# K/V token projections and output-gate projection placed inside the mLSTM chunk loop of a hybrid decoder layer

## What is computed

```python
proj = h @ w_in + b_in              # split: xin, bg, cg, q, k, v, o, ig, fg, gate_c, gate_m
y_conv = bg * causal_dwconv(cg * xin, conv_mix_w);  p_conv = y_conv @ w_proj_conv
# mLSTM, for each head and chunk, with decays from ig (exp) and fg (log_sigmoid):
#   C_next = s_old * C + sum_s w_s k_s v_s^T                  (state, carried from chunk to chunk)
#   num    = (tri * weights * q k^T) v + s_inter * (q C);     den: the same with v = 1
hm = num / max(|den|, exp(-m))      # then RMS norm over each head
hm = sigmoid(o) * rmsnorm(hm)
z = sigmoid(gate_c) * p_conv + sigmoid(gate_m) * (hm @ w_proj_mlstm)
x = x + gt1 * (z @ w_out)           # then a gated ConvFFN and a final norm
```

## Time and profile before

| | us |
|---|---|
| median of 2 runs | 1942.44 (1940.79 to 1944.08) |
| profiled execution | 1940.48 |
| its longest span, core 4, first to last instruction | 1939.2 |
| spans of the other seven cores | 1907.6 to 1935.8 |
| mean granted TensorE clock, core 4 | 0.857 of full |

### The profile page before, as it was taken

How to read it: one execution, slowest core, us unless ns; L and a number is a source line. 1 busy time by engine, 2 the same in 40 slices (tenths; PEclk the granted TensorE clock), 3 DMA queues, 4 the chain that set the end, 5 groups by cost and what they waited for, 6 DMA issues and landing times.

```text
span 1939.2 us, 25748 instructions; the slowest of 8 cores (1907.6 to 1939.2 us)
## 1 busy us (share of the span) xinstructions
PE 1494.9 (77%) x8664; PEld 802.5 (41%) x8664; DVE 950.2 (49%) x1746; ACT 651.0 (34%) x1436; POOL 118.0 (6%) x144
## 2 busy tenths in 40 slices
PE   0599649649987996297399979996296399979995
PEld 0254214325443443154256635553153255635553
DVE  0154472356245777123554356677123554256677
ACT  0253022533225333415422243323416322243333
POOL 1001000001000000100000000000100000100000
PEclk9699658759998998598599989998597599979998
DMA  4955932705776651927035594731936044684731
GB/s 96 166 137 94 156 66 44 109 1 84 112 121 108 93 83 44 205 45 109 1 52 80 88 171 62 114 56 59 209 47 100 1 66 66 100 154 72 110 55 66
DMA packets 142245, 174.54 MB, mean 90 GB/s; under 512 B 5155, under 2 KB 124963, under 8 KB 142117
## 3 DMA queue, kind: packets, MB, share of 16 engines
q0 software_dynamic: 131456, 136.86, 47.3%
q1 hardware_dynamic: 10662, 36.03, 5.5%
HBM read 301.35 MB, written 8.39 MB: 160 GB/s over the span
## 4 chain that ended last, share of the span: by engine, by line
PE 59%; DVE 14%; DMA 10%; issue 8%; ACT 7%; DVEq 1%; ACTq 0%; SPq 0%; POOLq 0%
PE psum L436 36%; PE psum L958 7%; PE psum L543 6%; DMA xt<-xin 3%; PE psum L535 3%; DMA wslot<-w_in 2%; DMA wslot<-w_ada 2%; PE psum L559 2%; PE psum L922 2%; ACT sqj L394 2%; DVE t3f L987 1%; DVE hm L789 1%; DVE C L562 1%; ACT t3f L985 1%; DVE actT L996 1%
## 5 line engine op out<-in xcount | busy, mean ns | idle before, releaser
L436 PE MATMUL psum<-hT,wslot 128*128 128x512 bf16 (+2 forms) x4800 | 773.9, 323 | 21.1 <-ACT hT L421 14.0
L436 PEld LDWEIGHTS psum<-hT,wslot 128*128 128x128 bf16 x4800 | 442.1, 100 | 340.3 <-issue 47.1
L958 PE MATMUL psum<-wslot,actT 128*128 128x512 bf16 x748 | 169.7, 388 | 22.4 <-DVE actT L996 22.0
L416 PE MATMUL psum<-identb,xnb 128*128 128x128 bf16 x392 | 38.6, 258 | 139.5 <-DVE stat L400 60.0
L961 DVE TENSOR_TENSOR x<-psum,x 128x512 f32<-128x512 f32 x204 | 133.9, 687 | 12.2 <-PE psum L958 1.2
L958 PEld LDWEIGHTS psum<-wslot,actT 128*128 128x128 bf16 x748 | 73.2, 99 | 116.1 <-issue 36.9
L894 ACT ACTIVATE sg<-psum,bcol 128x512 bf16<-128x512 f32 (+1 forms) x96 | 53.8, 563 | 177.4 <-PE psum L436 159.2
L978 ACT ACTIVATE a_s<-psum 128x512 f32<-128x512 f32 (+2 forms) x132 | 55.7, 470 | 150.9 <-DVE a_s L976 133.8
L991 ACT ACTIVATE sl<-t3f 128x768 f32<-128x768 f32 (+1 forms) x66 | 53.3, 808 | 142.6 <-DVE t3f L989 142.6
L119 POOL DMA_DIRECT2D wslot<-w_in x51 | 44.7, 883 | 913.5 <-PE psum L436 657.1
L416 PEld LDWEIGHTS psum<-identb,xnb 128*128 128x128 bf16 x392 | 29.5, 115 | 151.0 <-issue 150.8
(11 more groups left out here) (170 smaller groups left out, 1806.9 us busy)
## 6 DMA issues: line engine op xcount, KB each, us to landing
wslot<-w_in POOLq DMA_DIRECT2D x51, 1024.0 KB, 15.5
wslot<-w_up POOLq DMA_DIRECT2D x30, 1024.0 KB, 9.0
xt<-xin SPq DMA_DIRECT2D x49, 512.0 KB, 6.6
wslot<-w_down POOLq DMA_DIRECT2D x15, 1024.0 KB, 9.3
wslot<-w_ada POOLq DMA_DIRECT2D x12, 1024.0 KB, 24.1
y<-x SPq DMA_DIRECT2D x16, 512.0 KB, 2.7
wslot<-w_proj_conv POOLq DMA_DIRECT2D x6, 1024.0 KB, 11.7
wslot<-w_proj_mlstm POOLq DMA_DIRECT2D x6, 1024.0 KB, 10.8
```

The lines of the kernel that those rows point to most:

```text
L416: S.op("pe", lambda e, k=k, kk=kk: e.matmul(psum[:, b, kk * 128:(kk + 1) * 128], lhsT=xnb[i][:, k * 128:(k + 1) * 128], rhs=identb[:], sta ...
L436: S.op("pe", lambda e, k=k: e.matmul(psum[:, b, 0:n], lhsT=wslot[si][:, k, wcol0:wcol0 + 128], rhs=hT[:, k, t0:t0 + n], start=(k == 0), st ...
L958: S.op("pe", lambda e, jj=jj: e.matmul(psum[:, b, :], lhsT=actT[:, jj, c * 128:(c + 1) * 128], rhs=wd[:, jj, i * 512:(i + 1) * 512], start ...
```

## The change

In each stage the K/V block is taken apart. The 8 gate matmuls of each chunk stay ahead of `gate_math`, now in a loop of their own. The 24 matmuls of k and v (`kv_tok`) are issued for chunk 0 ahead of the output-gate units inside the gate stretch, and for chunk i+1 at the top of iteration i of the chunk loop. The output-gate units are cut finer: one for each 128 features and block of positions (16 instead of 8); 7 of the first block stay in the gate stretch, the other 9 are issued in the loop between `st_B` and `st_C2`: those that are due (the block holds the chunk) and, where there are any left, two more in each iteration. To leave banks 6 and 7 for this work, `st_B` uses 2 banks instead of 4 for its heads, with one ACT copy of 257 columns after each head instead of one of all four; the state update moves to banks 3 and 4 and the transposes to bank 5. The five weight slots of k, v and o are freed at the loop's end.

```diff
+        def gate_proj(hTt, r_hT, col0, gbank, ridx):
+            for k in range(8):
...
+        def kv_gate_proj(c, hTt, r_hT, col0, si_k, si_v, ktok, r_ktok, vaug, r_vaug, gbank, ridx, do_gate=True):
...
                     si_v = [load_w("w_in", O_V + i * 512) for i in range(2)]
+                    si_o = [load_w("w_in", O_O + i * 512) for i in range(2)]
                     for c in range(nch):
-                        kv_gate_proj(c, hT, r_hT[c], c * 128, si_k, si_v, ktok, r_ktok, vaug, r_vaug, gbank, c)
-                    free_w(si_k, *si_v)
+                        gate_proj(hT, r_hT[c], c * 128, gbank, c)
...
+                    def kv_tok(c):
+                        kv_gate_proj(c, hT, r_hT[c], c * 128, si_k, si_v, ktok, r_ktok, vaug, r_vaug, gbank, c, do_gate=False)
+                    o_units = []
+                    for (t0, n) in tbs:
+                        for j in range(8):
+                            def unit(t0=t0, n=n, j=j):
...
+                                fm_proj(si_o[j // 4], (j % 4) * 128, hT, r_hT, [(t0, n)], ev_o)
+                            o_units.append((t0 // 128, unit))
                     state["resv"] = {6, 7}
...
+                    pre_units = [lambda: kv_tok(0)] + [u_ for (_, u_) in o_units[:7]]
+                    o_units = o_units[7:]
+                    interleave(gate_math(ms, graw, r_graw, nch, first, True, (6, 7), gm), pre_units)
...
+                    def emit_o(due_chunk, extra):
+                        nonlocal_units = o_units
+                        while nonlocal_units and nonlocal_units[0][0] <= due_chunk:
+                            nonlocal_units.pop(0)[1]()
+                        for _ in range(extra):
+                            if nonlocal_units:
+                                nonlocal_units.pop(0)[1]()
+                    state["resv"] = {0, 1, 2, 3, 4, 5}
...
                         for h in range(4):
-                            S.op("pe", lambda e, h=h: e.matmul(psum[:, 1 + h, 0:257], lhsT=Sm[j][:, h, :], rhs=vaug[:, c, h, :], start=True, stop=False),
-                                 reads=[r_Sm[j], r_vaug[c]], writes=[r_X[h]], inc=False)
...
-                        S.op("act", lambda e: e.activation(out=Xs[j][:], in_=psum[:, 1:5, 0:257], func=AF.Copy), reads=r_X, writes=[r_Xs[j]])
-                        state_update(c, c * 4, ktok, r_ktok, vaug[:, c], r_vaug[c], sold, rg, (5, 6))
+                            xb = 1 + h % 2
+                            S.op("pe", lambda e, h=h: e.matmul(psum[:, xb, 0:257], lhsT=Sm[j][:, h, :], rhs=vaug[:, c, h, :], start=True, stop=False),
+                                 reads=[r_Sm[j], r_vaug[c]], writes=[r_X[h % 2]], inc=False)
+                            S.op("pe", lambda e, h=h: e.matmul(psum[:, xb, 0:257], lhsT=qT[:, h, cs], rhs=Cb[:, h, :], start=False, stop=True),
+                                 reads=[r_qT[c], r_Cb[h]], writes=[r_X[h % 2]])
+                            S.op("act", lambda e, h=h: e.activation(out=Xs[j][:, h, :], in_=psum[:, xb, 0:257], func=AF.Copy),
+                                 reads=[r_X[h % 2]], writes=[r_Xs[j]])
+                        state_update(c, c * 4, ktok, r_ktok, vaug[:, c], r_vaug[c], sold, rg, (3, 4))
...
                     for i in range(nch + 1):
                         if i + 1 < nch:
+                            kv_tok(i + 1)
                             prescale(i + 1)
                         if i < nch:
                             st_A(i)
                         if i >= 1:
                             st_C1(i - 1)
                         if i < nch:
                             st_B(i)
+                        emit_o(i, 2)
                         if i >= 1:
                             st_C2(i - 1)
                             st_D(i - 1)
+                    emit_o(nch, 99)
+                    free_w(si_k, *si_v)
+                    free_w(*si_o)
```

More of the change, by code:

```diff
@@ L530, in gate_math @@
             out.update(wG=wG, sold=sold, dmin=dmin, rg=rg)
-        def kv_gate_proj(c, hTt, r_hT, col0, si_k, si_v, ktok, r_ktok, vaug, r_vaug, gbank, ridx):
+        def gate_proj(hTt, r_hT, col0, gbank, ridx):
+            for k in range(8):
+                S.op("pe", lambda e, k=k: e.matmul(psum[:, gbank, ridx * 8:ridx * 8 + 8], lhsT=hTt[:, k, col0:col0 + 128], rhs=wgate[:, k, :],
+                                                  start=(k == 0), stop=(k == 7)),
+                     reads=[r_hT, r_wgate], writes=[r_bank[gbank]], inc=(k == 7))
+        def kv_gate_proj(c, hTt, r_hT, col0, si_k, si_v, ktok, r_ktok, vaug, r_vaug, gbank, ridx, do_gate=True):
             b = next_bank()
@@ L550, in kv_gate_proj @@
                      reads=[r_bank[b], r_par], writes=[r_vaug[ridx]])
[L551 to L554, removed]
+            if do_gate:
+                gate_proj(hTt, r_hT, col0, gbank, ridx)
         def state_update(ridx, gi0, ktok, r_ktok, vw, r_vw, sold, rg, pbank):
@@ L702, in run_stage @@
                          reads=[r_bank[gbank], r_par], writes=[r_graw])
-                    state["resv"] = {6, 7}
[L704 to L718, removed]
+                    def kv_tok(c):
+                        kv_gate_proj(c, hT, r_hT[c], c * 128, si_k, si_v, ktok, r_ktok, vaug, r_vaug, gbank, c, do_gate=False)
@@ new lines, in run_stage, with ev_o @@
+                    o_units = []
+                    for (t0, n) in tbs:
+                        for j in range(8):
+                            def unit(t0=t0, n=n, j=j):
+                                def ev_o(b, t0_, n_, j=j):
+                                    S.op("act", lambda e: e.activation(out=sgoT[:, j, t0_:t0_ + n_], in_=psum[:, b, 0:n_], func=AF.Sigmoid,
+                                                                       bias=bcol[:, 48 + j:49 + j]),
+                                         reads=[r_bank[b], r_par], writes=blk(r_sgoT, t0_, n_))
+                                fm_proj(si_o[j // 4], (j % 4) * 128, hT, r_hT, [(t0, n)], ev_o)
+                            o_units.append((t0 // 128, unit))
@@ L719, in run_stage @@
+                    state["resv"] = {6, 7}
                     gm = {}
-                    interleave(gate_math(ms, graw, r_graw, nch, first, True, (6, 7), gm), units)
+                    pre_units = [lambda: kv_tok(0)] + [u_ for (_, u_) in o_units[:7]]
+                    o_units = o_units[7:]
+                    interleave(gate_math(ms, graw, r_graw, nch, first, True, (6, 7), gm), pre_units)
                     wG, sold, dmin, rg = gm["wG"], gm["sold"], gm["dmin"], gm["rg"]
@@ L731, in run_stage @@
                     prescale(0)
-                    r_X = RL("X", 4)
+                    def emit_o(due_chunk, extra):
[6 more added lines that the diff above has]
+                    state["resv"] = {0, 1, 2, 3, 4, 5}
+                    r_X = RL("X", 2)
                     r_STb = Res("STb")
@@ L797, in st_D @@
                         for half in range(2):
-                            tb_ = 7
+                            tb_ = 5
                             for kk in range(4):
@@ L820, in run_stage @@
                             st_D(i - 1)
+                    emit_o(nch, 99)
+                    free_w(si_k, *si_v)
+                    free_w(*si_o)
+                    state["resv"] = set()
                     S.barrier()
```

2 lines of the change are left out of this document (removed).

## The result

| | us |
|---|---|
| median of 9 runs | 2004.94 (2000.44 to 2018.53) |
| the kernel before, beside it | 1942.27 (1938.72 to 1945.28), 8 runs |
| ratio | 1.032, 95% interval 1.0308 to 1.0331 |
| longest span of the profiled execution, core 5 | 2003.9 |
| forecast | 2014, range 1966 to 2060 |

The changed kernel is 62.7 us slower; +72 was forecast. In some executions of a kernel one die of the chip ran at a lower clock than the other; these are left out of the medians and ranges that follow, which is why some rest on one to three runs.

A forecast was written before the change was run, and what follows sets the result against it. PE's matmuls bound the K/V blocks, the chain the gate stretch, waits the loop. Terms: 162.1 in, 90.0 out, +72 us on the 1939.2 span gives 2011; plus 1.3 and 2.0, 2014 us, range 1966 to 2060.

The forecast's parts named there:

- all three items on which it would have been wrong: Loop signs: prescale waits under 1 us; state update no later behind the square root; clock near 0.5 or 1.0.
- bursts in iteration 0 (3): K/V matmuls in each loop's first iteration, after the gate stretch's idle tail: 7.1 us each.
- bursts in iteration 1 (3): K/V matmuls right behind output units that have raised the clock: 5.1 us each.
- bursts behind two units (6): K/V matmuls behind two output units and transposes, clock taken as midway: 6.25 us each.
- two banks: In st_B, head 2 waits for head 0's ACT copy behind the square root: +2.5 us in 14 iterations, 36.1 in all.
- new table loads: Sigmoids in the loop make the next square root reload its table: 7 x 1.28 = 9.0 us.
- output units in the loop: Unhidden in iteration 0, partly hidden later by the wait before the transposes: 30.4 us, bounds 18 and 42.
- out: K/V block less gate matmuls: Front of the stages: 91.6 us of K/V blocks go, 7.8 us of gate matmuls stay, 83.8 us saved.
- out: gate stretch: Shorter units and sigmoids against added kv_tok(0): about -1.0 us per 6 chunks, -4.2 for 5, -6.2 together.
- Full clock throughout: Loop: PE's clock stays full since it has more to do; +24, 1966 us; chance 0.13.
- Half clock throughout: Loop: the clock never rises inside it; +138, 2081 us; chance 0.10.
- Real overlap: Loop: new work fills PE's idle time, a burst costing only its DVE copies; -16, 1927 us; chance 0.05.

The follow-up runs named there:

- banks_only: The kernel before with only st_B put on two PSUM banks, one ACT copy after each head: 1974.72 us, ratio 1.0161.
- the last version: The run fill: changed kernel with K/V in three groups where PE waits, later DVE copies and a reordered loop; 1897.45 us, ratio 0.9777.
- o_dense: The changed kernel with all 16 output-gate units in the gate stretch, none in the loop: 2007.32 us, ratio 1.0322.
- fill: Changed kernel, K/V in three groups where PE waits, copies later, loop reordered, output units in gate stretch: 1897.45 us, ratio 0.9777; rerun 1889.51 and 1890.7.
- fill_dense: The run fill with all K/V projections in one block ahead of the gate stretch, the rest kept: 1954.28 us, ratio 1.0067.

## Why the forecast was right, and where its sizes were off

The direction, the mechanisms and all three items on which it would have been wrong came out as foretold: `prescale` waited for the copies of the burst, the state update moved behind the square root, and the loop's clock stood at 0.70. The terms, forecast against measured in the changed kernel's rows (for the bursts the forecast is the cost, length less 0.1 us, and the measured value the length):

| term | forecast | measured |
|---|---|---|
| bursts in iteration 0 (3) | 21.3 | 7.14 + 6.87 + 7.94 = 21.9 |
| bursts in iteration 1 (3) | 15.3 | 3 x 5.18 = 15.5 |
| bursts behind two units (6) | 37.5 | 5 x 5.18 + 6.99 = 32.9 |
| the stage of 5: the other two | 12.5 | 5.18 + 6.55 = 11.7 |
| two banks | 36.1 | 14 x 2.39 = 33.5 (iteration 0 under 0.2 each) |
| new table loads | 9.0 | 7 x 1.28 = 9.0 |
| the three loads of before, now on the chain | 0 | 3 x 1.17 = 3.5 |
| output units in the loop | 30.4 | 15.8 + 1.8 + 9.5 = 27.1 |
| in, sum | 162.1 | 155.1 |
| out: K/V block less gate matmuls | 83.8 | 91.6 - 3.4 = 88.2 |
| out: gate stretch | 6.2 | 3.4 + 1.5 + 1.1 = 6.0 |
| net | +72 | +61 by terms; spans +64.7, medians +62.7 |

**Bursts.** The term that was mis-sized upward: "the six behind two units and transposes 6.25, midway". Five of the six ran at full clock, 5.18. I had put them between two rows; what the changed timeline shows is that behind the 16 matmuls of the units and the transposes (from 947.56 to the next burst at 952.66, with one idle stretch of 0.94) the clock is up when the burst begins. The sixth, in the second stage of 6 (1531.26 to 1538.25), took 6.99 behind the same units; why is open. The run with all units in the gate stretch shows the other side: behind the first of each loop, bursts of 6.2 to 7.8 us. So -4.6 us here, and -0.8 in the stage of 5.

**Gate matmuls alone.** 7.8 us came from their weight loads inside the K/V block, 8 in 0.46, 57 ns each. Alone, 48 matmuls with their 48 loads take 1.35 us (867.12 to 868.47), 28 ns each: 4.4 us less over the three stages. The row gave the pace of loads with other matmuls around them.

**A term put at nothing.** "Before there was one such load in a loop": the sum counts only the seven new ones. In the kernel before, that one load was hidden, as the earlier trace rows shows together with the state update beside it:

```profile
911.29 0.88 DVE L562 SCALAR_TENSOR_TENSOR C<-C,g_sold,psum 128x257 f32<-128x257 f32 x2 [1.83 <-PE psum L559]
```

The state update began 0.42 us ahead of the load (911.71). In the changed kernel the same load stands before the copy of head 0, and the state update comes behind both:

```profile
922.62 1.28 ACT L796 ACT_TABLE_LOAD   x1
...
925.88 0.87 DVE L566 SCALAR_TENSOR_TENSOR C<-C,g_sold,psum 128x257 f32<-128x257 f32 x2 [5.50 <-PE psum L563]
```

By banks_only that costs 1.17 us in each loop. Both changes, banks and sigmoids, were priced; what the first does to the old load was not.

**Banks, new loads, units, gate stretch** hold within 3.3 us each. For the load, the row decided rightly: it ends at 944.39 and the square root starts at 944.41, and 1.28 for each is what the periods have room for (20.49 us above is made up with it). The Trainium skill (ScalarE: Activation LUTs, "What ACT_TABLE_LOAD costs") has 2.66 us with its drain; the trace does not agree with it here.

**What no term holds.** The windows say +52.3, +52.0 and +53.2 for the three loops, the terms 51.4, 51.0 and 52.8. These 2.3 us (3.7 with the bursts taken at their cost) are not assigned. Another 1.4 us of the spans' difference lie outside the three parts. So the net of the forecast was 7 us above the spans' difference and 11 above the terms read: bursts, gate matmuls, units and banks were priced 15 us too high in sum, and the old loads 3.5 too low. That the total came as near as it did is in part such errors cancelling.

**Rivals.** Full clock throughout (1966): its price for the later bursts was right, but iteration 0 and the loop's small matmuls stayed at half pace. Half clock throughout (2081): fell, five of six bursts. Real overlap (1927): fell in this kernel, since with k and v in a block it was 3 to 11 us faster and not slower. But the last version shows that its premise was sound. PE's idle time can hold k and v whole, for a result 2.2 to 2.8% below the kernel before. The Trainium skill (Perfetto Trace Analysis, "Optimization Strategy") says that interleaving regimes with different contended engines may gain; here interleaving gave +3.2% in one place and -2.2% in another, so the trace agrees with it only where the place is chosen by the gaps.

## What to carry to other kernels

An idle share of 60% says how much PE waits, not where. Before moving work into a loop of waits, take one iteration's timeline, mark where the engine waits for another one, and issue the work directly ahead of that waiting instruction, with its evictions on the other engine at a point where that one has slack; in front of the iteration, where both queues were ready, the same matmuls cost all of their time and more. Count the resources that the moved work takes from the loop: here two PSUM banks cost half of the loss by themselves, because they made a matmul wait for a copy that stood behind a square root, and in one iteration of each loop behind its table load, in an in-order queue. And when a gap is filled, look at the clock as well, for the loop's own work speeds up with it.

## What the hardware did that I had not expected

- The clock of a burst depends on what PE did just before, though not on that alone. Identical bursts of 24 matmuls took 5.18 us in five of six cases behind 16 matmuls of output units and transposes (6.99 in the sixth), 6.87 us where 1.35 us of idle time preceded the transposes, and 7.84 us behind a loop iteration without units (run o_dense).
- Filling gaps can pay twice (runs fill and fill_dense). An iteration with 24 more matmuls and three more DVE copies took 10.91 us at granted clock 1.00, the same iteration without them 11.67 us at 0.50.
- Matmuls of 8 columns, each with its own weight load of 128 by 128, went at 28 ns each (48 of them in 1.35 us).
- A table load cost 1.28 us and a gap of 0.02 us behind it, also where it alternated with another table in each iteration: 10 such loads for the square root where there were 3.
